# End of the first feed-forward: operand parts ahead of the squares, and the next stage's first unit copied unscaled

## Chip, cores and metric

The kernel runs on one core of one Trainium2 chip. The metric is the device time of one execution in microseconds (us), as the median of several runs. The engines are called PE (matmul; PEld is its weight load), DVE (VectorE), ACT (ScalarE), POOL (GpSimd) and SP (which here only issues DMAs).

## What is computed

Two transformer blocks follow each other on one sequence of 1024 tokens with 1024 features, all in fp32. The change touches the seam between them, where the first block's feed-forward ends, its last norm is taken, and the second block's input projection begins:

```python
        h2 = rmsnorm(x, norm_ffn[l])
        gate, up = jnp.split(h2 @ w_ffn_in[l], 2, axis=-1)
        x = x + (jax.nn.silu(gate) * up) @ w_ffn_out[l]
    return rmsnorm(x, norm_final)
...
    for l in range(DEPTH):
        a = rmsnorm_2(x, norm_pre_mix[l])
        mix = token_mixer(a, cos, sin, w_in[l], b_gates[l], conv_w[l], conv_b[l], ml_head_norm[l],
                          q_norm[l], w_uq[l], kv_norm[l], w_ukv[l], w_out[l])
...
def token_mixer(a, cos, sin, w_in, b_gates, conv_w, conv_b, ml_head_norm,
                q_norm, w_uq, kv_norm, w_ukv, w_out):
    proj = a @ w_in
```

## The kernel before

Activations lie transposed: `acc` holds x as eight tiles of 128 features by 1024 tokens. Every fp32 product is made of three matmuls on split operands: high weight part by high operand part, high by low, low by high. The high part of an operand is a rounded copy, the low part is the value less the high part.

**The feed-forward's output.** It is done in "pairs" of output tiles by a Strassen-like scheme of seven products (`r` = 0 to 6). The last pair is `P1_LAST`. `output_dve` adds the products into `acc`; `f1_act` makes high weight parts and, between them, squares.

**The seam.** `FIN = (5, 6, 7, 0, 1, 2, 4, 3)` is the order in which the tiles of `acc` are finished; number n of it is called "tile n" here (0 to 7). Each tile needs four things:

- `fin_squares` (ACT): two squares, one plain into `sq_a`, one with the last norm's gain into `sq_b`. Each buffer exists once, so a square waits until DVE has added the one before it.
- `fin_add` (DVE): the "A add" of `sq_a` into `sq_sum_a`, and the "B add" of `sq_b` into `sq_sum_b`.
- `fin_hi` (ACT): the high operand part `g1hi`.
- `fin_lo` (DVE): the low operand part `g1lo`.

`fin_pe` sums the squares over the features by matmuls with ones (`ones,sq_sum_a`, then `ones,sq_sum_b`). `fin_means` (DVE) turns the sums into means and reciprocals, and writes them on diagonals. `fin_spread` (PE) spreads these over the partitions, and `fin_act` takes the roots `r1` (tile name `lat_r`) and `rstd`. The two norms follow each other, so one pair of sums serves both.

**The next stage.** `in2` projects in 17 "units" of one output tile each, 48 matmuls of 128x512, in the order of `IN2_ORDER`. Unit 0 has buffers of its own for its weights; the others alternate between two. `split_unit` makes a unit's high and low weight parts on POOL and waits until the unit two before it is done on PE. `store_dve` multiplies a unit's result in PSUM by `rstd` into `stage`, which frees the PSUM banks; `store_act` stores it. `fin_dve` then scales the eight tiles of `acc` (L2310), `spill2_act` writes all of `acc` to HBM as one DMA (`x_block<-acc`), and SP waits for that DMA in `gates_sp` before it issues six small loads and then the weights of unit 5:

```python
                if j == 4:
                    gates_sp(sp)
...
        def gates_sp(sp):
            sp.wait_ge(S["x_spilled"], 32)
            sp.wait_ge(S["stored"][U_IN2 % 2], stored2(0))
```

The order on each engine is the order of the code; engines meet at semaphores only.

Of the kernel before, what the change touches and what calls it, by code (L numbers as in the profile page):

```python
# [18 lines left out]
ALU = mybir.AluOpType  # L19
# [178 lines left out]
def parted(m):  # L198

    return PARTED_TO[m]  # L200
# [99 lines left out]
def two_block_kernel(nc, A, out):  # L300
# [34 lines left out]
    with ctx:  # L335
# [1702 lines left out]
        def f1_act(act):  # L2038
# [32 lines left out]
            for p in range(2, P2):  # L2071
                first_act(act, p)
                for i in range(7):
                    pair_act(act, p, i)
                    change_act(act, p, i)
                    if p < P1O and p % 2 == 0 and i in (3, 4, 5):
                        silu_act(act, p // 2, i - 3)
                    if P1_LAST - 3 < p and i in (1, 4):
                        fin_squares(act, 2 * (p - P1_LAST + 2) + i // 4)
                if p < P1O and p % 2 == 0:  # L2080
                    silu_act(act, p // 2, 3)
            for n in range(KT):
                fin_hi(act, n)
# [51 lines left out]
        def f1_dve(dve):  # L2135
# [35 lines left out]
            for n in range(4, KT):  # L2171
                fin_lo(dve, n)
            for n in (KT - 2, KT - 1):
                fin_add(dve, n)
# [76 lines left out]
        def fin_act(act):  # L2251
            for n in (KT - 2, KT - 1):
                fin_squares(act, n)
            f = 2 * NORM_AT["final"]
            act.wait_ge(S["norm_sum"], f + 3)
            act.activation(r1, PS[2][:, :], ACT.Sqrt).then_inc(S["rstd_ready"], 1)
            act.wait_ge(S["norm_sum"], f + 4)
            act.activation(rstd[:, :], PS[3][:, :], ACT.Sqrt).then_inc(S["rstd_ready"], 1)

        def in2_weights_pool(pool, i):  # L2260
# [9 lines left out]
            else:  # L2270
                pool.wait_ge(*count("sw_lo", parted(AT[P1_LAST, 6])))
                pool.wait_ge(*count("s_product", done(P1_LAST, 3)))
                split_unit(pool, u)

# [28 lines left out]

        FIN0 = KT + 3

# [66 lines left out]
        def in2_pe(pe):  # L2372
            pe.wait_ge(*count("s_post", posted(P1_LAST - 1, "12")))
            for j in range(N_IN2):
                if j == 0:
                    mm_unit(pe, Step(U_IN2), g1hi, g1lo, ks=FIN, w=(whi_in2, wlo_in2), wait_k=lambda k:
                            pe.wait_ge(S["lo_ready"], OPERAND["mix2"] + FIN.index(k) + 1))
                else:
                    mm_unit(pe, Step(U_IN2 + j), g1hi, g1lo,
                            wait_k=(lambda k: fin_spread(pe) if k == 3 else None) if j == 1 else None)  # L2380
                if j == 0:
                    fin_pe(pe)
                if j == 8:
# [16 lines left out]
        def in2_act(act):  # L2400
            for j in range(N_IN2):
                t = IN2_ORDER[j]
                store_act(act, Step(U_IN2 + j), proj2[t * P:(t + 1) * P, :])
                if j == 0:
                    spill2_act(act)
                if j == 2:
                    gates_act(act)
# [27 lines left out]
        def in2_dve(dve):  # L2435
            dve.wait_ge(S["rstd_ready"], NORM_AT["mix2"] + 1)
            for j in range(N_IN2):
                store_dve(dve, Step(U_IN2 + j), U_IN2, B2)
                if j == 0:
                    fin_dve(dve)  # L2440
# [1578 lines left out]
        def output_dve(dve, p):  # L4019
# [52 lines left out]
            next_lo(dve, p, 3)  # L4072
            if P1_LAST - 3 < p < P2:
                fin_add(dve, 2 * (p - P1_LAST + 2))
            if N_PAIR - 4 < p:
                end_adds(dve, p - 1)
# [17 lines left out]
            next_lo(dve, p, 5)  # L4094
            if p == P1_LAST:
                for n in range(3):
                    fin_lo(dve, n)
            change_dve(dve, p, 6)
# [5 lines left out]
            change_dve(dve, p, 7)  # L4104
            if P1_LAST - 3 < p < P2:
                fin_add(dve, 2 * (p - P1_LAST + 2) + 1)
# [303 lines left out]
```

## Time and profile before

| what | value |
|---|---|
| median of 3 runs | 2695.09 us (2694.74 to 2695.11) |
| profiled execution, own time | 2693.12 us |
| span of the profile | 2691.4 us |
| mean granted PE clock, share of full | 0.994 |
| busy: PE, DVE, POOL, ACT | 2595.1, 1857.9, 1224.1, 1042.9 us |

The span runs from the first to the last instruction. Times in the rows are from the span's start. A row's brackets give the idle time of that engine just before, and what ended it.

### The profile page before, as it was taken

The numbers are of one execution on the slowest core, as the hardware profiler recorded it, in microseconds if no ns is written. First come the engines' busy times: TensorE is split into PE (matmuls) and PEld (weight loads), VectorE is DVE, ScalarE is ACT, GpSimd is POOL, SyncE is SP. The second block draws the span as 40 slices with busy tenths as digits, with TensorE's granted clock in tenths as the row PEclk, the third lists the DMA queues.
The fourth block names the chain that finished last, engine by engine and source line by source line (L and its number), as shares of the span: only waits on it lengthen the run. The fifth ranks groups of instructions, "written<-read, shape, count | busy, mean of one in ns | idle before, by whom it ended". The sixth has DMA issues, their size and how long they took to land.

```text
span 2691.4 us, 32407 instructions
## 1 busy us (share of the span) xinstructions
PE 2595.1 (96%) x12366; PEld 2089.7 (78%) x12366; DVE 1857.9 (69%) x2108; ACT 1042.9 (39%) x1447; POOL 1224.1 (45%) x763
## 2 busy tenths in 40 slices
PE   7999999999999999999998999989998999999998
PEld 5888787887777888887886788656885888877777
DVE  7565665457658666668879647766558666778887
ACT  5223343323124333234435111756555433434444
POOL 2222222233447888884333433241135888723331
PEclk9999999999999999999999999999999999999999
DMA  5333333244332433245641343401323554754543
GB/s 192 118 102 114 121 94 126 83 152 155 130 130 63 118 102 111 81 133 199 215 137 55 132 152 101 126 1 46 131 83 84 172 155 147 220 156 160 164 141 141
DMA packets 335840, 339.49 MB, mean 126 GB/s; under 512 B 19723, under 2 KB 254838, under 8 KB 335686
## 3 DMA queue, kind: packets, MB, share of 16 engines
q1 hardware_dynamic: 329446, 313.81, 37.3%
q10 hardware_dynamic: 6240, 23.59, 2.3%
q8 instruction: 100, 1.64, 0.2%
q14 instruction: 54, 0.44, 0.1%
HBM read 228.55 MB, written 107.77 MB: 125 GB/s over the span
## 4 chain that ended last, share of the span: by engine, by line
PE 52%; DVE 10%; issue 2%; ACT 1%; DMA 1%; POOL 1%; SPq 0%; DVEq 0%; ACTq 0%; POOLq 0%
PE ps L3712 36%; PE ps L566 9%; DVE op_lo L3789 2%; PE ps L2784 2%; PE ps L2807 1%; DVE sw_lo L3622 1%; PE ps L2794 1%; DVE acc L4033 1%; DVE acc L4040 1%; PE ps L3288 1%; DVE acc L2310 0%; DVE x L2731 0%; DMA x_block<-acc 0%; DVE op_lo L3692 0%; PE ps L3673 0%
## 5 line engine op out<-in xcount | busy, mean ns | idle before, releaser
L3712 PE MATMUL ps<-op_hi,sw_hi 128*128 128x512 f32 x1769 | 693.2, 392 | 15.8 <-DVE op_lo L3789 8.4
L3712 PE MATMUL ps<-op_hi,sw_lo 128*128 128x512 f32 x1769 | 689.7, 390 | 0.0
L3712 PE MATMUL ps<-op_lo,sw_hi 128*128 128x512 f32 x1769 | 689.5, 390 | 0.0
L3712 PEld LDWEIGHTS ps<-op_hi,sw_hi 128*128 128x128 f32 x1769 | 332.8, 188 | 96.6 <-issue 16.7
L3712 PEld LDWEIGHTS ps<-op_hi,sw_lo 128*128 128x128 f32 x1769 | 332.8, 188 | 69.7
L3712 PEld LDWEIGHTS ps<-op_lo,sw_hi 128*128 128x128 f32 x1769 | 333.0, 188 | 68.9 <-issue 0.5
L532 POOL TENSOR_TENSOR w_hi_t<-w_raw,ones 128x1024 fp32r<-128x1024 f32 (+1 forms) x60 | 118.5, 1978 | 531.1 <-DMA w_raw<-in_w_in 238.0
L3612 ACT ACTIVATE sw_hi<-sw_sumNone 128x512 fp32r<-128x512 f32 (+1 forms) x252 | 157.1, 624 | 332.2 <-PE ps L3712 250.0
L3622 POOL TENSOR_TENSOR sw_lo<-sw_sumNone,sw_hi 128x512 fp32r<-128x512 f32 x138 | 213.8, 1559 | 34.2 <-ACT sw_hi L3612 34.1
L3573 POOL TENSOR_TENSOR sw_sumNone<-sw_raw 128x512 f32<-128x512 f32 (+1 forms) x63 | 113.8, 1806 | 232.1 <-DVE sw_lo L3622 209.3
L3612 ACT ACTIVATE sw_hi<-sw_raw 128x512 fp32r<-128x512 f32 (+1 forms) x189 | 117.5, 622 | 198.1 <-PE ps L3712 196.4
L3622 POOL TENSOR_TENSOR sw_lo<-sw_raw,sw_hi 128x512 fp32r<-128x512 f32 x109 | 159.2, 1462 | 54.7 <-ACT sw_hi L3612 54.7
L536 POOL TENSOR_TENSOR w_lo_t<-w_raw,w_hi_t 128x1024 fp32r<-128x1024 f32 (+1 forms) x60 | 156.3, 2609 | 4.2
L674 DVE TENSOR_TENSOR stage<-ps,rstd 128x1024 f32<-128x1024 f32 x37 | 45.1, 1219 | 125.3 <-PE ps L566 110.1
L3588 POOL TENSOR_TENSOR sw_sumNone<-sw_raw,sw_sumNone 128x512 f32<-128x512 f32 (+1 forms) x63 | 91.7, 1456 | 87.5 <-DVE sw_lo L3622 84.8
L3744 DVE TENSOR_TENSOR hidden_blocks<-ps,s_u 128x512 f32<-128x512 f32 x111 | 76.1, 686 | 77.4 <-PE ps L3712 76.9
L3580 POOL TENSOR_TENSOR sw_sumNone<-sw_sumNone,sw_raw 128x512 f32<-128x512 f32 (+1 forms) x63 | 98.7, 1566 | 61.8 <-DVE sw_lo L3622 59.0
L3728 DVE TENSOR_TENSOR s_u<-ps,s_p 128x512 f32<-128x512 f32 x65 | 44.8, 689 | 116.3 <-PE ps L3712 111.1
L3789 DVE TENSOR_TENSOR op_lo<-op_raw,op_hi 128x2048 fp32r<-128x2048 f32 (+1 forms) x49 | 119.1, 2433 | 7.2 <-ACT op_hi L3782 7.2
L566 PE MATMUL ps<-m2hi,w_hi_t 128*128 128x512 f32 x304 | 106.1, 405 | 3.7 <-DVE m2lo L1450 2.1
L566 PE MATMUL ps<-h1hi,w_hi_t 128*128 128x512 f32 x320 | 103.7, 405 | 4.0 <-DVE stage L674 4.0
L566 PE MATMUL ps<-m2lo,w_hi_t 128*128 128x512 f32 x304 | 101.7, 390 | 0.0
(500 smaller groups left out, 5423.5 us busy)
## 6 DMA issues: line engine op xcount, KB each, us to landing
op_raw<-hidden SPq DMA_DIRECT2D x42, 1024.0 KB, 8.7
w_raw<-in_w_in SPq DMA_DIRECT2D x47, 512.0 KB, 4.6
sw_raw<-in_w_ffn_in SPq DMA_DIRECT2D x44, 512.0 KB, 5.2
hidden<-hidden_blocks SPq DMA_DIRECT2D x13, 1536.0 KB, 6.1
hidden<-hidden_blocks SPq DMA_DIRECT2D x14, 1280.0 KB, 5.0
sw_raw<-in_w_up SPq DMA_DIRECT2D x32, 512.0 KB, 8.6
sw_raw<-in_w_down SPq DMA_DIRECT2D x32, 512.0 KB, 5.5
acc<-proj SPq DMA_DIRECT2D x30, 512.0 KB, 4.5
```

The lines of the kernel that those rows point to most:

```text
L532: ins = pool.tensor_tensor(whi[:, u.par, s], raw[:, u.par, s], ones[:, 0:1].to_broadcast([P, n]), ALU.mult)
L536: ins = pool.tensor_tensor(wlo[:, u.par, s], raw[:, u.par, s], whi[:, u.par, s].bitcast(F32), ALU.subtract)
L566: mm = pe.matmul(out[:, b * HALF:(b + 1) * HALF], w, x[:, k, b * HALF:(b + 1) * HALF], start=(begin and k == ks[0] and n == 0), stop=(end ...
L2784: mm = pe.matmul(PS[n % 2][:, b:b + w], qT[0:96, h, i * P:(i + 1) * P], kT[0:96, h, b:b + w], start=True, stop=True)
L3573: pool.tensor_tensor(s1, a21, a22, ALU.add).then_inc(S["sw_sum"], 1)
L3580: pool.tensor_tensor(s2, s1, a11, ALU.subtract).then_inc(S["sw_sum"], 1)
L3588: pool.tensor_tensor(s2, a12, s2, ALU.subtract).then_inc(S["sw_sum"], 1)
L3612: act.activation(wshi[ring(m)][:, 0:n], weight_block(p, r), ACT.Copy).then_inc(S["sw_hi"], 1)
L3622: eng.tensor_tensor(wslo[ring(m)][:, 0:n], weight_block(p, r), wshi[ring(m)][:, 0:n].bitcast(F32), ALU.subtract).then_inc(S["sw_lo"], 1)
L3712: mm = pe.matmul(out, w, x[:, k, :], start=(k == 0 and i == 0 and r < 4), stop=(k == n - 1 and i == 2), skip_group_check=r >= 4)
L3744: dve.tensor_tensor(out, bank(p, r), u[:, :], ALU.add).then_inc(S["s_post"], 1)
L3789: dve.tensor_tensor(lo_of(first, r)[:, :, :], fresh_of(first, r)[:, :, :], hi_of(first, r)[:, :, :].bitcast(F32), ALU.subtract).then_inc(S ...
```

## The change

On ACT, the high parts of the first three tiles are made inside the last pair, where tile 4's squares stood. After the pair come tile 4's squares, the high weight part of unit 1 (which POOL made before; POOL now only makes its low part), the other five high parts, and then the squares of tiles 5 to 7. On DVE, the first three low parts follow the third addition of the last pair, where tile 4's adds stood; the other five follow the pair's end, and all adds of tiles 4 to 7 come behind them. On PE, the sums stand no longer between units 0 and 1 but ahead of the sixth of unit 1's eight contraction steps, and the spreads ahead of the second step of unit 2 instead of the fourth of unit 1. Unit 0 is copied unscaled from PSUM by ACT (`in2_copy`); DVE scales it in `stage` later (`in2_scaled`), after it has stored unit 1 and before `fin_dve`.

```diff
-                    if P1_LAST - 3 < p and i in (1, 4):
+                    if P1_LAST - 3 < p < P1_LAST and i in (1, 4):
                         fin_squares(act, 2 * (p - P1_LAST + 2) + i // 4)
+                    if (p, i) == (P1_LAST, 1):
+                        for n in range(3):
+                            fin_hi(act, n)
                 if p < P1O and p % 2 == 0:
                     silu_act(act, p // 2, 3)
-            for n in range(KT):
+            fin_squares(act, 4)
+            in2_weights_act(act)
+            for n in range(3, KT):
                 fin_hi(act, n)
...
             for n in range(4, KT):
                 fin_lo(dve, n)
-            for n in (KT - 2, KT - 1):
+            for n in range(4, KT):
                 fin_add(dve, n)
...
         def fin_act(act):
-            for n in (KT - 2, KT - 1):
+            for n in range(5, KT):
                 fin_squares(act, n)
+            in2_copy(act)
...
-                pool.wait_ge(*count("sw_lo", parted(AT[P1_LAST, 6])))
-                pool.wait_ge(*count("s_product", done(P1_LAST, 3)))
-                split_unit(pool, u)
+                split_lo(pool, u)
+
+        def in2_weights_act(act):
+            act.wait_ge(S["w_split"], U_IN2 + 1)
+            act.wait_ge(*count("sw_lo", parted(AT[P1_LAST, 6])))
+            act.wait_ge(*count("s_product", done(P1_LAST, 3)))
+            split_hi(act, Step(U_IN2 + 1))
+
+        def in2_copy(act):
+
+            u = Step(U_IN2)
+            act.wait_ge(S["unit_done"], U_IN2 + 1)
+            act.wait_ge(S["stored"][u.par], stores_before(u, U_IN2, B2) * 16)
+            act.activation(stage[:, u.par, :], PS[u.par][:, :], ACT.Copy).then_inc(S["unit_out"][u.par], 1)
+
+        def in2_scaled(dve):
+
+            u = Step(U_IN2)
+            dve.wait_ge(S["unit_out"][u.par], u.nth())
+            dve.tensor_tensor(stage[:, u.par, :], stage[:, u.par, :], rstd[:, :], ALU.mult).then_inc(S["fin_done"], 1)
...
                     mm_unit(pe, Step(U_IN2 + j), g1hi, g1lo,
-                            wait_k=(lambda k: fin_spread(pe) if k == 3 else None) if j == 1 else None)
-                if j == 0:
-                    fin_pe(pe)
+                            wait_k={1: lambda k: fin_pe(pe) if k == 5 else None,
+                                    2: lambda k: fin_spread(pe) if k == 1 else None}.get(j))
...
-                store_act(act, Step(U_IN2 + j), proj2[t * P:(t + 1) * P, :])
                 if j == 0:
+                    u = Step(U_IN2)
+                    act.wait_ge(S["fin_done"], FIN0)
+                    act.dma_start(proj2[t * P:(t + 1) * P, :], stage[:, u.par, :]).then_inc(S["stored"][u.par], 16)
                     spill2_act(act)
+                else:
+                    store_act(act, Step(U_IN2 + j), proj2[t * P:(t + 1) * P, :])
...
-            for j in range(N_IN2):
+            for j in range(1, N_IN2):
                 store_dve(dve, Step(U_IN2 + j), U_IN2, B2)
-                if j == 0:
+                if j == 1:
+                    in2_scaled(dve)
                     fin_dve(dve)
...
-            if P1_LAST - 3 < p < P2:
+            if P1_LAST - 3 < p < P1_LAST:
                 fin_add(dve, 2 * (p - P1_LAST + 2))
+            if p == P1_LAST:
+                for n in range(3):
+                    fin_lo(dve, n)
...
-            if p == P1_LAST:
-                for n in range(3):
-                    fin_lo(dve, n)
...
-            if P1_LAST - 3 < p < P2:
+            if P1_LAST - 3 < p < P1_LAST:
                 fin_add(dve, 2 * (p - P1_LAST + 2) + 1)
```

`split_hi` and `split_lo` are there before; `split_hi` is one ACT copy of 128x1024, `split_lo` one subtraction of that size on POOL. `FIN0` grows by one for the new step.

Three places of the order on the engines follow. The first is DVE at the end of the last pair, from tile 4's adds to the last adds; `acc<-ps,acc` are the pair's additions, `g1lo` the low parts, `sq_sum_a` and `sq_sum_b` the adds. Before:

```order
L2243 TENSOR_TENSOR sq_sum_a<-sq_sum_a,sq_a 128x1024
L2249 TENSOR_TENSOR sq_sum_b<-sq_sum_b,sq_b 128x1024
L4040 TENSOR_TENSOR acc<-ps,acc 128x512 x2
L2232 SCALAR_TENSOR_TENSOR g1lo<-acc,gg,g1hi 128x1024 x3
L4040 TENSOR_TENSOR acc<-ps,acc 128x512
L2243 TENSOR_TENSOR sq_sum_a<-sq_sum_a,sq_a 128x1024
L2249 TENSOR_TENSOR sq_sum_b<-sq_sum_b,sq_b 128x1024
L2232 SCALAR_TENSOR_TENSOR g1lo<-acc,gg,g1hi 128x1024 x5
L2243 TENSOR_TENSOR sq_sum_a<-sq_sum_a,sq_a 128x1024
L2249 TENSOR_TENSOR sq_sum_b<-sq_sum_b,sq_b 128x1024
L2243 TENSOR_TENSOR sq_sum_a<-sq_sum_a,sq_a 128x1024
L2249 TENSOR_TENSOR sq_sum_b<-sq_sum_b,sq_b 128x1024
```

The same place after the change, from the third addition of the last pair on:

```order
L4067 TENSOR_TENSOR acc<-ps,acc 128x512
L2237 SCALAR_TENSOR_TENSOR g1lo<-acc,gg,g1hi 128x1024 x3
L4067 TENSOR_TENSOR acc<-ps,acc 128x512 x3
L2237 SCALAR_TENSOR_TENSOR g1lo<-acc,gg,g1hi 128x1024 x5
L2248 TENSOR_TENSOR sq_sum_a<-sq_sum_a,sq_a 128x1024
L2254 TENSOR_TENSOR sq_sum_b<-sq_sum_b,sq_b 128x1024
L2248 TENSOR_TENSOR sq_sum_a<-sq_sum_a,sq_a 128x1024
L2254 TENSOR_TENSOR sq_sum_b<-sq_sum_b,sq_b 128x1024
L2248 TENSOR_TENSOR sq_sum_a<-sq_sum_a,sq_a 128x1024
L2254 TENSOR_TENSOR sq_sum_b<-sq_sum_b,sq_b 128x1024
L2248 TENSOR_TENSOR sq_sum_a<-sq_sum_a,sq_a 128x1024
L2254 TENSOR_TENSOR sq_sum_b<-sq_sum_b,sq_b 128x1024
```

The low parts moved to the front and all eight adds to the back; how many of each there are is unchanged.

The second place is DVE at the first stores of `in2`, from the second diagonal on; `stage<-ps,rstd` is `store_dve`, `acc<-acc,cols,lat_r` is `fin_dve`. Before:

```order
L614 TENSOR_TENSOR lat_r<-ident,bytok 128x1024
L674 TENSOR_TENSOR stage<-ps,rstd 128x1024
L2310 SCALAR_TENSOR_TENSOR acc<-acc,cols,lat_r 128x1024 x8
L674 TENSOR_TENSOR stage<-ps,rstd 128x1024 x3
L2562 MEMSET ssq 4x1024
```

After the change:

```order
L614 TENSOR_TENSOR lat_r<-ident,bytok 128x1024
L674 TENSOR_TENSOR stage<-ps,rstd 128x1024
L2296 TENSOR_TENSOR stage<-stage,rstd 128x1024
L2333 SCALAR_TENSOR_TENSOR acc<-acc,cols,lat_r 128x1024 x8
L674 TENSOR_TENSOR stage<-ps,rstd 128x1024 x2
L2589 MEMSET ssq 4x1024
```

One row is new, L2296, ahead of the eight; the store ahead of it is now unit 1's.

The third place is ACT from the last pair's middle on; `sw_hi_106` is the last high weight part of the feed-forward, `w_hi_t` unit 1's. After the change:

```order
L2231 ACTIVATE g1hi<-acc,gg 128x1024 x3
L3639 ACTIVATE sw_hi_106<-sw_sumNone_122 128x384
L2222 ACTIVATE sq_a<-acc 128x1024
L2224 ACTIVATE sq_b<-acc,cols 128x1024
L542 ACTIVATE w_hi_t<-w_raw 128x1024
L2231 ACTIVATE g1hi<-acc,gg 128x1024 x5
L2222 ACTIVATE sq_a<-acc 128x1024
L2224 ACTIVATE sq_b<-acc,cols 128x1024
L2222 ACTIVATE sq_a<-acc 128x1024
L2224 ACTIVATE sq_b<-acc,cols 128x1024
L2222 ACTIVATE sq_a<-acc 128x1024
L2224 ACTIVATE sq_b<-acc,cols 128x1024
```

Before, all eight high parts stood together behind the squares of tiles 4 and 5, and there was no row for `w_hi_t`.

## Rows read from the trace of the kernel before

**Rows 1.** Page of the profile: busy time, share, instructions of the matmul engine

```profile
PE 2595.1 (96%) x12366; PEld 2089.7 (78%) x12366; DVE 1857.9 (69%) x2108; ACT 1042.9 (39%) x1447; POOL 1224.1 (45%) x763
```

**Rows 2.** Timeline of PE, 1455 to 1520: start, duration (us), what, [idle before, releaser]

```profile
1466.61 0.39 PE L3712 MATMUL ps<-op_hi,sw_lo 128*128 128x512 f32 x1
...
1473.50 1.19 PE L566 MATMUL ps<-g1hi,w_hi_in 128*128 128x512 f32 x2 [6.50 <-DVE g1lo L2232]
...
1479.86 0.73 PE L566 MATMUL ps<-g1hi,w_hi_in 128*128 128x512 f32 x2 [0.59 <-DVE g1lo L2232]
...
1488.19 2.05 PE L602 MATMUL ps<-ones,sq_sum_a 128*128 128x128 f32 x16 [1.24 <-DVE sq_sum_a L2243]
...
1491.02 2.05 PE L602 MATMUL ps<-ones,sq_sum_b 128*128 128x128 f32 x16 [0.78 <-DVE sq_sum_b L2249]
...
1492.83 0.71 PE L566 MATMUL ps<-g1hi,w_hi_t 128*128 128x512 f32 x2
...
1497.01 1.88 PE L608 MATMUL ps<-ssq,ones 128*128 128x512 f32 x4
```

**Rows 3.** Timeline of DVE, 1455 to 1520

```profile
1464.32 2.12 DVE L2243 TENSOR_TENSOR sq_sum_a<-sq_sum_a,sq_a 128x1024 f32<-128x1024 f32 x1
...
1466.37 3.38 DVE L2249 TENSOR_TENSOR sq_sum_b<-sq_sum_b,sq_b 128x1024 f32<-128x1024 f32 x1
...
1472.07 3.67 DVE L2232 SCALAR_TENSOR_TENSOR g1lo<-acc,gg,g1hi 128x1024 fp32r<-128x1024 f32 x3 [1.13 <-ACT g1hi L2226]
...
1478.53 6.06 DVE L2232 SCALAR_TENSOR_TENSOR g1lo<-acc,gg,g1hi 128x1024 fp32r<-128x1024 f32 x5
...
1486.91 1.22 DVE L2243 TENSOR_TENSOR sq_sum_a<-sq_sum_a,sq_a 128x1024 f32<-128x1024 f32 x1
...
1501.70 1.23 DVE L674 TENSOR_TENSOR stage<-ps,rstd 128x1024 f32<-128x1024 f32 x1 [5.39 <-ACT rstd L2258]
...
1502.84 13.46 DVE L2310 SCALAR_TENSOR_TENSOR acc<-acc,cols,lat_r 128x1024 f32<-128x1024 f32 x8
```

**Rows 4.** Timeline of POOL, 1430 to 1600

```profile
1463.09 2.28 POOL L532 TENSOR_TENSOR w_hi_t<-w_raw,ones 128x1024 fp32r<-128x1024 f32 x1 [6.10 <-DVE sw_lo L3622]
...
1465.45 3.21 POOL L536 TENSOR_TENSOR w_lo_t<-w_raw,w_hi_t 128x1024 fp32r<-128x1024 f32 x1
...
1487.10 2.78 POOL L532 TENSOR_TENSOR w_hi_t<-w_raw,ones 128x1024 fp32r<-128x1024 f32 x1 [18.44 <-PE ps L566]
...
1509.03 2.86 POOL L532 TENSOR_TENSOR w_hi_t<-w_raw,ones 128x1024 fp32r<-128x1024 f32 x1
...
1518.44 1.89 POOL L532 TENSOR_TENSOR w_hi_t<-w_raw,ones 128x1024 fp32r<-128x1024 f32 x1 [3.23 <-PE ps L566]
...
1520.42 2.39 POOL L536 TENSOR_TENSOR w_lo_t<-w_raw,w_hi_t 128x1024 fp32r<-128x1024 f32 x1
```

**Rows 5.** Timeline of ACT, 1455 to 1520

```profile
1470.84 8.41 ACT L2226 ACTIVATE g1hi<-acc,gg 128x1024 fp32r<-128x1024 f32 x8
```

**Rows 6.** Chain that ended last, 1500 to 1760: start, us, what

```profile
1516.33 11.73 DMA x_block<-acc
...
1531.30 4.10 DMA w_raw<-in_w_in
...
1535.47 2.38 POOL w_hi_t L532
...
1540.36 43.81 PE ps L566 x192
```

**Rows 7.** Timeline of PE: two other waits of over 2 us

```profile
750.97 0.72 PE L566 MATMUL ps<-m1hi,w_hi_t 128*128 128x512 f32 x2 [2.59 <-POOL w_lo_t L536]
...
1267.86 0.47 PE L3712 MATMUL ps<-op_hi,sw_hi 128*128 128x512 f32 x1 [2.54 <-DVE op_lo L3789]
```

**Rows 8.** Stretches: PEclk is the granted clock, 1.00 is full

```profile
1268.50:1271.90 3.40, 3.40 (x10) 2.62 (x9) 2.32 (x3) 0.00 (x0) 1.28 (x1) 0.51 1.11 344
...
1470.00:1476.50 6.50, 3.00 (x7) 2.48 (x8) 5.37 (x7) 6.50 (x7) 0.00 (x0) 0.50 0.27 76
```

More of the change, by code:

```diff
@@ L2302, in fin_means @@
             diagonal(dve, ssq2, 1).then_inc(S["norm_mean"], 2)
-        FIN0 = KT + 3
+        FIN0 = KT + 4
         def fin_dve(dve):
```

## Prediction

> **What bounds the kernel now.** The page comes first: PE is busy 2595.1 of 2691.4 us [rows 1], so a time saved elsewhere counts only where PE waits. The timeline of PE shows where it does at the seam. The feed-forward ends at 1466.61 + 0.39 = 1467.0, and PE then stands idle for 6.50 us, until DVE has the first low part. There follow 0.59 us before tile 3, 1.24 us before the A sums and 0.78 us before the B sums [rows 2], 9.1 us in all. After the wait the granted clock is at 0.50, which is 1.2 GHz, from 1470 to 1476.5 [rows 8]; some 3 us of work at half clock cost another 1.6.
>
> The timeline of DVE says why the low parts are late: tile 4's adds start at 1464.32 and 1466.37 and take 2.12 and 3.38 us [rows 3] where such an add takes 1.22 (1486.91). POOL is splitting unit 1's weights from 1463.09 to 1465.37 and from 1465.45 to 1468.66 [rows 4]; each add ends 1.1 us after POOL's instruction, so it had stood still until POOL was through. The eight scalings of `fin_dve` show the same: 13.46 us [rows 3], where eight at the 1.2 us of a low part (6.06 for five) make 9.6; POOL's 1509.03 and the one behind it fall into them [rows 4]. A split that waits for nobody holds DVE for 1.89 + 2.39 = 4.28 us (1518.44 and 1520.42) [rows 4].
>
> The chain of waits gives the last thing to read, and it decides. `fin_dve` ends at 1516.3, the write of `acc` starts at 1516.33 and lands 11.7 us later, SP issues its small loads, unit 5's weights land from 1531.30 on, POOL splits them at 1535.47, and PE starts unit 5 at 1540.36 [rows 6]. So unit 5 starts 24.03 us after `fin_dve` is done, however early PE gets there. PE came only 0.3 us too early: units 3 and 4 are 48 matmuls each, 10.9 us a unit (1540.36 + 43.81 for 192, which are four), and unit 2 was done when POOL started at 1518.44 [rows 4, 6], so unit 4 was done at about 1540.1.
>
> **Part by part.** First, PE's stall. With the first high parts made inside the last pair, the first low part needs only DVE, free at 1464.32. ACT makes unit 1's high weights when DVE has parted the last feed-forward weights, which released POOL at 1463.09 [rows 4]; at 8.41/8 = 1.05 us a copy [rows 5] POOL can take the low part at 1464.25. It may hold DVE for 2.39 us; if DVE gets in first, the second low part is held instead. In the first case low parts 0 to 2 end at 1467.9, 1469.1 and 1470.2; three additions of 0.6 us (my reading of the 0.6 between such rows) bring 1472.0, and low part 3 ends at 1473.3. PE starts at 1467.95, waits 1.3 us before tile 3, and from there needs what it needed before, 1479.86 to 1487.0 [rows 2]: unit 0 is done at 1480.4, 6.6 us earlier. Both waits are short; I take no fall of the clock there.
>
> Second, the sums. PE reaches the sixth step of unit 1 at 1480.4 + 5 x 1.36 = 1487.2 (6 matmuls of 0.227 us a step, from 43.81/192). When is the last A add done? Between 1464.32 and that add DVE does the same work before and after: eight low parts, three additions, seven adds. Before it ended at 1486.91 + 1.22 = 1488.13, and the stretch held three waits: 0.9 and 2.2 us for POOL, 1.13 idle [rows 3], 4.2 in all. Now it holds unit 1's low part, 2.39, and, because unit 0 is done at 1480.4, unit 2's whole split, 4.28, which before started at 1487.10 [rows 4], behind all but one add: 6.67, less nothing idle, since ACT's squares for tiles 5 to 7 take turns with the adds and hide beside them (0.1 us at most). The last A add ends 6.67 - 4.2 = **2.5 us later**, at 1490.6, and PE stands idle for 3.4 us before the sums.
>
> Third, the spreads. Sums cost 1.81 us each (1491.02 to 1492.83) [rows 2]. Before, from the last A add to the spreads: 1497.01 - 1488.13 = 8.9. Now: two sums 3.6, then four steps 5.45, and a start of 0.1: 9.1. The B adds and the diagonals fit beside the four steps. **+0.2**.
>
> Fourth, roots to the write. The spreads to `rstd` stay 1497.01 to 1501.70 [rows 2, 3]. DVE then stores unit 1 (1.14, as unit 0 before), scales unit 0, which is new: **+1.14**, and runs the eight scalings. Unit 3's split is over by then, but unit 4's starts when unit 2 is done, about 6 us into the eight, just where unit 3's fell before, so they keep 13.46. `in2_copy` (1 us on ACT) hides beside the sums on PE. The Trainium skill bears on this edit ("SBUF — State Buffer", "SBUF: two separate sides"): a DVE instruction with two SBUF inputs and a POOL instruction exclude each other for the whole instruction. By that rule the scaling in `stage`, unlike the one from PSUM, could be held by a split, up to 4.28 us more if it met one; I count no hold, as POOL is free then by the rows.
>
> So `fin_dve` ends 2.5 + 0.2 + 1.14 = **3.84 us later**, and with it unit 5's start. What PE gained is spent in front of unit 5, where it now stands idle for some 9 us.
>
> Fifth, the clock. Of two waits of like length, 2.54 us was followed by 3.4 us at 0.51 and 2.59 us by none [rows 7, 8]. For the 3.4 us before the sums the price is 0 or 3.4/2 = 1.7; I take **+1.7**, the longer wait being nearer to the fall. For the 9 us before unit 5 a fall is as good as certain; what it costs lies between 0 (the clock is back as the work starts) and 3.4 (the whole 6.5 us at 0.50 on work); I take what the 6.50 us wait cost, **+1.6**.
>
> Sum: 3.84 + 1.7 + 1.6 = +7.1 us on the profiled execution's own 2693.12 (its span is 2691.4), 2700.2. The median of the runs lies 1.97 above it, 2695.09, so **2702.2**, 0.26% slower. Behind unit 5 everything hangs on PE and moves with it.
>
> **The rivals.** What a measurement of this kernel can tell from no change is about 0.2%, 5.4 us: 2689.7 to 2700.5.
>
> *Late write, cheap clock.* The same chain, but the clock holds at the sums, or is back when unit 5 starts: +3.8 to +5.5, 2698.9 to 2700.6. For it stands the 2.59 us wait without a fall. Chance 0.28.
>
> *POOL's split does not meet the adds.* If the adds slip through between POOL's instructions, the last A add ends at 1486.1 and PE is not held: the spreads come at 1487.2 + 9.1 = 1496.3, 0.7 earlier, the scaling takes its 1.14, and the write starts 0.5 later; with the clock's 1.6, +2.1, 2697.2. Against it stand all four held DVE rows. Chance 0.1.
>
> *The write is not what unit 5 waits for* (the other side). If the 24.03 us from write to unit 5 shrank by 9 us or more, PE's own progress would count: after the sums PE has done 6.8 us more work than at 1492.83, and it is there at 1490.6 + 3.6 = 1494.2: 5.4 us gained, less 0 to 1.7 for the clock, so 2689.7 to 2691.4. The 0.3 us with which unit 5 waited before speaks for a balance of the two; but nothing in the change touches the DMA, the small loads or POOL's split. Below 9 us of shrinking the gain is less, and over 0.2% it is only if the A adds come earlier too. Chance 0.07.
>
> **How the numbers follow.** The forecast, late write with both falls of the clock, has 0.52 and its own range 2700.6 to 2704.6 (1.8 us more than forecast if the second fall costs 3.4, and 0.6 for the terms before it). 0.03 is left for a worse meeting of splits with the scalings (+4.3 more). The range reaches down to the third case: 2697.0 to 2704.6. Slower by over 0.2%: 0.52 + 0.03 = 0.55. Within: 0.28 + 0.1 and 0.02 of the last rival = 0.4. Faster: the other 0.05 of it.
>
> **What the changed profile would show.** Right: PE's wait before unit 0 falls from 6.50 us to about 1; unit 2's split on POOL starts near 1480.5, and an A and a B add beside it are held for about 2 us each; the A sums start near 1490.6 after an idle time of about 3 us; the write of `acc` starts at 1520 to 1522; PE idles 9 to 10 us before unit 5, released by POOL's low part, at 1544 to 1546, with a clock of 0.50 around it. Wrong: a write before 1516.3, or a unit 5 that waits for nothing. The step that I trust least is the meeting of POOL's and DVE's instructions, since an order that differs by 0.1 us moves 2 us.

## The result, and the profile after

The changed kernel takes 2701.07 us, the median of 17 runs (2697.52 to 2703.15), against 2694.74 us for 17 runs of the kernel before on the same chip: ratio 1.0024, 95% interval 1.0017 to 1.0031, so 6.3 us slower. 2702.2 was predicted. A profile is of one execution and need not be the median's: this one is of the fastest of the 17.

The timeline of PE in the profile after (own time 2697.52 us) answers to [rows 2]:

```profile
1461.57 0.50 PE L3739 MATMUL ps<-op_hi,sw_hi 128*128 128x512 f32 x1 [0.53 <-DVE s_u L3762]
...
1466.84 0.70 PE L566 MATMUL ps<-g1hi,w_hi_in 128*128 128x512 f32 x2 [0.89 <-DVE g1lo L2237]
...
1472.13 0.73 PE L566 MATMUL ps<-g1hi,w_hi_in 128*128 128x512 f32 x2 [0.93 <-DVE g1lo L2237]
...
1489.05 2.05 PE L602 MATMUL ps<-ones,sq_sum_a 128*128 128x128 f32 x16 [3.02 <-DVE sq_sum_a L2248]
1490.94 1.95 PE L602 MATMUL ps<-ones,sq_sum_b 128*128 128x128 f32 x16
...
1498.19 1.88 PE L608 MATMUL ps<-ssq,ones 128*128 128x512 f32 x4
...
1542.24 1.22 PE L566 MATMUL ps<-g1hi,w_hi_t 128*128 128x512 f32 x2 [9.16 <-POOL w_lo_t L536]
```

The stall before unit 0 has shrunk from 6.50 to 0.89 us, and two others have grown: 3.02 us before the A sums and 9.16 us before unit 5, which was 0.30 us before. To compare executions I count from the first row here, the last pair's matmul that waits for `s_u`. Call it R. It comes between 1459.9 and 1464.3 in the profiles of this document, whatever the kernel, so times from the span's start can't be laid beside each other. It and the end of the stretch read so in the kernel before (the timelines of PE and of POOL):

```profile
1462.60 0.50 PE L3712 MATMUL ps<-op_hi,sw_hi 128*128 128x512 f32 x1 [0.54 <-DVE s_u L3735]
```

```profile
1551.68 2.08 POOL L532 TENSOR_TENSOR w_hi_t<-w_raw,ones 128x1024 fp32r<-128x1024 f32 x1 [4.21 <-PE ps L566]
```

The second row is POOL's start on unit 7, which PE releases by finishing unit 5: 89.08 us after R. DVE after, which answers to [rows 3]:

```profile
1463.30 5.79 DVE L2237 SCALAR_TENSOR_TENSOR g1lo<-acc,gg,g1hi 128x1024 fp32r<-128x1024 f32 x3
...
1480.35 2.89 DVE L2254 TENSOR_TENSOR sq_sum_b<-sq_sum_b,sq_b 128x1024 f32<-128x1024 f32 x1
1483.17 3.42 DVE L2248 TENSOR_TENSOR sq_sum_a<-sq_sum_a,sq_a 128x1024 f32<-128x1024 f32 x1
...
1487.77 1.23 DVE L2248 TENSOR_TENSOR sq_sum_a<-sq_sum_a,sq_a 128x1024 f32<-128x1024 f32 x1
...
1502.88 1.23 DVE L674 TENSOR_TENSOR stage<-ps,rstd 128x1024 f32<-128x1024 f32 x1 [7.82 <-ACT rstd L2264]
1504.03 1.22 DVE L2296 TENSOR_TENSOR stage<-stage,rstd 128x1024 f32<-128x1024 f32 x1
1505.16 13.43 DVE L2333 SCALAR_TENSOR_TENSOR acc<-acc,cols,lat_r 128x1024 f32<-128x1024 f32 x8
```

And POOL after, which answers to [rows 4]:

```profile
1463.20 2.40 POOL L546 TENSOR_TENSOR w_lo_t<-w_raw,w_hi_t 128x1024 fp32r<-128x1024 f32 x1 [7.24 <-ACT w_hi_t L542]
1479.38 2.79 POOL L532 TENSOR_TENSOR w_hi_t<-w_raw,ones 128x1024 fp32r<-128x1024 f32 x1 [13.77 <-PE ps L566]
1482.24 3.26 POOL L536 TENSOR_TENSOR w_lo_t<-w_raw,w_hi_t 128x1024 fp32r<-128x1024 f32 x1
...
1511.47 2.70 POOL L532 TENSOR_TENSOR w_hi_t<-w_raw,ones 128x1024 fp32r<-128x1024 f32 x1 [8.66 <-PE ps L566]
1514.25 3.25 POOL L536 TENSOR_TENSOR w_lo_t<-w_raw,w_hi_t 128x1024 fp32r<-128x1024 f32 x1
1537.54 1.89 POOL L532 TENSOR_TENSOR w_hi_t<-w_raw,ones 128x1024 fp32r<-128x1024 f32 x1 [20.03 <-DMA w_raw<-in_w_in]
...
1555.30 1.89 POOL L532 TENSOR_TENSOR w_hi_t<-w_raw,ones 128x1024 fp32r<-128x1024 f32 x1 [5.93 <-PE ps L566]
```

Laid over each other, these two show the mechanism. POOL's split of unit 2 starts at 1479.38 because unit 0 is done then, and beside it a B add takes 2.89 us and an A add 3.42 us where the undisturbed one takes 1.23. POOL's own two take 2.79 and 3.26 us there. The chain that ended last, after, goes where that of before went [rows 6]:

```profile
1518.62 11.75 DMA x_block<-acc
...
1533.61 3.87 DMA w_raw<-in_w_in
...
1537.54 1.89 POOL w_hi_t L532
...
1539.51 2.68 POOL w_lo_t L536
...
1542.24 45.55 PE ps L566 x192
```

The stretch from R to the end of unit 5 now takes 1555.30 - 1461.57 = 93.73 us, 4.65 more than before; this profiled execution has no fall of the clock at the sums. Where those 4.65 us come from is plain in PE's waits and its clock: before 6.50 + 0.59 + 1.24 + 0.78 + 0.30 and 1.6 for half clock, 11.0 us; after 0.89 + 0.93 + 3.02 + 9.16 and 1.74, 15.7 us. The rest, PE's work, is the same 78 us in both.

### The profile page after: what moved, and what is told of

Read it like the earlier page. It is cut to its first block, busy times and chain, and to the rows that moved or that the text cites. A ratio compares the mean times of both kernels' runs of the same rounds, so it can differ in the third digit from the quotient of the medians.

```text
span 2695.8 us, 32408 instructions
## 1 busy us (share of the span) xinstructions
PE 2595.4 (96%) x12366; PEld 2090.2 (78%) x12366; DVE 1854.4 (69%) x2108; ACT 1045.7 (39%) x1449; POOL 1219.1 (45%) x762
## 4 chain that ended last, share of the span: by engine, by line
PE 53%; DVE 9%; issue 2%; DMA 2%; ACT 1%; POOL 1%; SPq 0%; DVEq 0%; ACTq 0%; POOLq 0%
PE ps L3739 36%; PE ps L566 9%; DVE op_lo L3816 2%; PE ps L2811 2%; PE ps L2834 1%; PE ps L2821 1%; DVE sw_lo L3649 1%; DMA op_raw<-hidden 1%; PE ps L3315 1%; DVE acc L4060 1%; DVE acc L4067 0%; DVE x L2758 0%; DVE acc L2333 0%; DMA x_block<-acc 0%; DVE sq_sum_a L2248 0%
```

## The experiments

Two theories stood against each other. **W**: unit 5's start hangs on the write of `acc`, so only what moves the write counts. **S**: the loss is the new wait at the sums with its half clock, and the write is a bystander. The table gives what the profiles show, all from R: when the write of `acc` is issued, when unit 5 starts and how long PE had waited for it, when unit 5 is done; the last column is the median less that of before in the same batch.

| kernel | wait at A sums | write | unit 5 (wait) | unit 5 done | median, us |
|---|---|---|---|---|---|
| before | 1.24 | 53.73 | 77.76 (0.30) | 89.08 | |
| changed | 3.02 | 57.05 | 80.67 (9.16) | 93.73 | +6.33 |
| e10, changed again | 3.01, clock falls | 58.49 | 82.17 (9.22) | 94.84 | +6.85 |
| e3, unit 2's split held | 0 | 53.78 | 77.73 (9.49) | 91.55 | +1.91 |
| e1, unit 4's split held | 2.98, clock falls | 54.91 | 78.52 (5.37) | 91.52 | +3.31 |
| e12, both held | 0 | 49.97 | 73.64 (5.44) | 87.58 | -1.56 |
| e8, first half alone | 9.77, clock falls | 55.96 | no wait | 90.99 | +1.88 |
| e9, before, write held | 1.23 | 56.75 | 80.42 (2.93) | 94.51 | +3.49 |
| e11, first half, waits moved | 6.05, clock falls | 48.91 | no wait | 87.44 | -0.63 |
| e5, all waits moved | 0 | 49.96 | no wait | 79.22 | -10.94 |

**e1: unit 4's split held until the eight scalings are done.** In `in2_pool`:

```diff
+                if j == 4:
+                    pool.wait_ge(S["fin_done"], FIN0 + KT)
                 if j >= 2:
                     split_unit(pool, Step(U_IN2 + j))
```

> The changed kernel, with POOL's split of unit 4's weights held back until the eight scalings of fin_dve are done. Nothing ahead of the scalings moves, PE's 3.0 us wait before the sums included. Theory W (unit 5 starts a fixed 23.6 us after the write of acc is issued, and the cost is that the write comes later): the scalings take 9.4 us instead of 13.4, the write is issued at about 1514.6 instead of 1518.6, PE's wait before unit 5 shrinks from 9.2 to about 5.2 us, and the time falls by 4.0 us against the changed kernel, to 2.3 us above before (ratio 1.0008). Theory S (the cost is PE's own wait and low clock at the sums, and the wait before unit 5 only shows time already lost): no change, 6.3 us above before (1.0024).

2697.84 us, ratio 1.0011 (1.0003 to 1.0020): 3.0 us less than the changed kernel lost, where W had said 4.0. DVE's timeline:

```profile
1507.53 9.65 DVE L2333 SCALAR_TENSOR_TENSOR acc<-acc,cols,lat_r 128x1024 f32<-128x1024 f32 x8
```

The scalings fall from 13.43 to 9.65 us, the wait before unit 5 from 9.16 to 5.37, by the same 3.8. The wait at the sums is the same 2.98 us, and here the clock did fall, seen in the length of the A sums' row on PE:

```profile
1489.78 3.68 PE L602 MATMUL ps<-ones,sq_sum_a 128*128 128x128 f32 x16 [2.98 <-DVE sq_sum_a L2248]
```

Half the loss goes though nothing at the sums became better: for W, against S.

**e3: unit 2's split held until the adds are done**, `if j == 2: pool.wait_ge(S["fin_done"], KT)` at the same place.

> The changed kernel, with POOL's split of unit 2's weights held back until the last B add. Theory W: the adds are no longer held, the last A add ends at about 1485.1 instead of 1489.0, PE goes from unit 1's fifth step into the sums without its 3.0 us wait, the spreads and the write come 3.0 us earlier (write at 1515.6), and the time falls by 3.0 us, and by up to 1.7 more where the clock fell at the sums: 1.6 to 3.3 us above before (1.0006 to 1.0012), with some 6 us of wait left before unit 5 and more of PE's gain unused. Theory S: the wait at the sums was the cost, so with it gone the kernel is as fast as before or faster (1.0000 or less).

2696.44 us, ratio 1.0005 (0.9997 to 1.0014). PE's timeline (A sums, unit 5):

```profile
1488.67 1.95 PE L602 MATMUL ps<-ones,sq_sum_a 128*128 128x128 f32 x16
...
1542.07 1.22 PE L566 MATMUL ps<-g1hi,w_hi_t 128*128 128x512 f32 x2 [9.49 <-POOL w_lo_t L536]
```

No wait at the sums at all, so POOL's split was the whole of it, and yet PE waits 9.49 us before unit 5. Counted from R the write (53.78) and unit 5 (77.73) are where they were in the kernel before (53.73, 77.76): what PE gained earlier is handed back to within 0.1 us. W had said some 6 us of wait; it stays at 9, since PE reaches unit 5 earlier by as much as the write comes earlier. The 2.47 us that are left until unit 5 is done are the half clock after that wait. S asked for a ratio of 1.0000 or less here, and the time doesn't exclude it: of the eleven executions five took 2693.1 to 2694.0 us and six 2696.4 to 2698.8. The profile, of the slowest, speaks against S; what the five faster ones lacked no profile shows.

**e8: the first half of the change alone.** Operand parts ahead of the squares as in the change, but the sums between units 0 and 1, the spreads in unit 1, and unit 0 stored from PSUM, as before.

```diff
-            in2_copy(act)
...
-                            wait_k={1: lambda k: fin_pe(pe) if k == 5 else None,
-                                    2: lambda k: fin_spread(pe) if k == 1 else None}.get(j))
+                            wait_k=(lambda k: fin_spread(pe) if k == 3 else None) if j == 1 else None)
+                if j == 0:
+                    fin_pe(pe)
```

> The first half of the change alone: operand parts ahead of the squares, unit 1's high weights on ACT; but the sums stay between units 0 and 1, the spreads ahead of unit 1's fourth step, and DVE scales and stores unit 0 from PSUM as before. Theory W: the last A add comes as late as in the changed kernel, so PE waits about 10 us before the sums; from there two sums and three steps to the spreads, and no scaling in stage: the write comes 1.2 us later than before, 2.9 with a fall of the clock at the sums, and so does the end: 1.0004 to 1.0011. What the changed kernel loses beyond this is the price of the second half. If earlier operand parts help by themselves, it is faster than before.

2696.76 us, ratio 1.0008 (0.9999 to 1.0017). PE's timeline:

```profile
1488.19 3.48 PE L602 MATMUL ps<-ones,sq_sum_a 128*128 128x128 f32 x16 [9.77 <-DVE sq_sum_a L2248]
```

The last A add is as late as in the whole change (27.4 us after R in both), so the first half already spends PE's gain: it waits the 9 us at the sums instead of at unit 5. The second half moves that wait behind the write and makes the write later by 2.5 us (58.49 in e10 against 55.96): 1.1 for the scaling in `stage`, 1.4 for one contraction step more between the sums and the spreads, four instead of three. It costs 4.4 us by the medians (of two batches). By the stretch to unit 5's end it costs 3.9 (94.84, e10, which like e8 has the clock's fall at the sums); 93.73, without the fall, would give 2.7.

**e2: the kernel before with unit 3's split held** until the scalings are done (`j == 3`, the split that meets them there).

> The kernel before, with POOL's split of unit 3's weights held back until the eight scalings are done. The write of acc is issued about 4 us earlier, at 1512.3 instead of 1516.3. Theory W with PE only 0.3 us early at unit 5: at most 0.3 us is gained (ratio 0.9999), since PE's own progress takes over; the 0.3 us wait before unit 5 is gone. If the write's time counted alone in the kernel before too: 4 us gained (0.9985).

2692.74 us, ratio 0.9995 (0.9986 to 1.0004). The scalings take 9.68 us, the write comes 49.99 us after R instead of 53.73, and unit 5 waits for nothing. It is done 88.51 us after R instead of 89.08, 0.6 us earlier, where the wait that it had to gain was 0.3, and the ratio's interval holds 1. In the kernel before, write and PE were in balance, which is why a write 3.3 us later shows and one 3.7 us earlier doesn't.

**e4: unit 5's weights ahead of the small loads.** In `in2_sp` of the changed kernel:

```diff
-                if j == 4:
+                if j == 5:
                     gates_sp(sp)
```

> The changed kernel, with SP loading unit 5's weights ahead of its wait for the write of acc and the six small loads, which now stand ahead of unit 6's weights. The write itself stays where it is. Theory W: unit 5 starts at about 1533 without a wait. DVE's chain on the small loads (the gates, then the store of unit 4, which ended at 1548.3) is the next thing that hangs on the write: unit 6 waits for it until about 1548.4, instead of starting near 1554.6; with a clock fall after that shorter wait 5 to 6 us are gained on the changed kernel, which puts it 0.3 to 1.5 us above before (1.0001 to 1.0006). Theory S: nothing is gained, 1.0024.

2698.04 us, ratio 1.0013 (1.0004 to 1.0022): direction right, size above what W said. The wait before unit 5 is gone, but the gate work on DVE, which waits for the small loads and so now stands later, is still ahead of unit 4's store, and unit 6 writes into the buffer which that store empties:

```profile
1552.21 0.71 PE L566 MATMUL ps<-g1hi,w_hi_t 128*128 128x512 f32 x2 [3.65 <-DVE stage L674]
```

In its profile unit 5's 9.2 us have become 3.65 here, and the stretch is 0.9 us longer than before (1599.13 less R at 1464.28, against 1596.51 less 1462.60, the same start of POOL four units on); the median says 3.5, where W had said 0.3 to 1.5. The profile is of this kernel's slowest execution, which lost another 4.9 us behind the seam, with more falls of the clock there: the mean granted clock is 0.90 in the 50 us from 250 us after R and 0.97 in those from 900 us on, where it was 0.97 and 1.00 before. Why, I did not find out.

**e6: the gate work of the kernel before one unit later**, on all three engines:

```diff
-                if j == 4:
+                if j == 5:
                     gates_sp(sp)
...
-                if j == 2:
+                if j == 3:
                     gates_act(act)
...
-                if j == 3:
+                if j == 4:
                     gates_dve(dve)
-                if j == 4:
+                if j == 5:
                     rows_dve(dve)
```

> The kernel before with only the moves of the small loads and of the work on them (unit 5's weights first, the work one unit later on ACT and DVE), and nothing of the change. Theory W: PE's own progress bounds it, so only the 0.3 us wait before unit 5 goes: 0.9999, within 0.03% of before. If these moves alone made the gain of a kernel that has them all, it shows here: 0.997.

2693.88 us, ratio 0.9995 (0.9986 to 1.0004). The interval holds W's 0.9999 and not the 0.997 of the other case. In the profile the last 0.3 us of waiting goes, and unit 5 is done 88.51 us after R as in e2. The hold of e2 and these moves were not run together on the kernel before; each alone leaves PE nothing to wait for up to unit 5's end.

**e5: the changed kernel with everything that W names removed**: both holds (e1, e3) and the three moves of e6.

> The changed kernel with both splits held back (unit 2's until the last B add, unit 4's until the eight scalings are done), unit 5's weights loaded ahead of the small loads, and the work on the small loads one unit later on ACT and DVE (behind the stores of units 3 and 4, its second part behind unit 5's), so that no store of a unit stands behind it. Theory W: the waits before the sums, before unit 5 and before unit 6 are all gone, the write is issued at about 1511.5, and PE runs without a wait of over 0.5 us from unit 0's fourth step to the end of the 17 units; unit 6 starts some 9 us earlier than in the kernel before. 7 to 10 us faster than before (ratio 0.9963 to 0.9974). If something else than the write and its chain holds the units (DMA bandwidth, POOL's splits), less than 4 us are gained.

2683.94 us, the median of five executions, ratio 0.9963 (0.9950 to 0.9975): 10.9 us less than before, slightly more than W gave, where the changed kernel took 6.3 more: 17.2 us (0.6%) between the two. PE's timeline of the whole stretch holds these waits and no other:

```profile
1466.04 0.70 PE L566 MATMUL ps<-g1hi,w_hi_in 128*128 128x512 f32 x2 [0.88 <-DVE g1lo L2237]
...
1471.33 0.73 PE L566 MATMUL ps<-g1hi,w_hi_in 128*128 128x512 f32 x2 [0.95 <-DVE g1lo L2237]
...
1485.07 1.95 PE L602 MATMUL ps<-ones,sq_sum_a 128*128 128x128 f32 x16
```

and its table by stretches says the same of the clock (PEclk, third column from the end):

```profile
1460.00:1545.00 85.00, 82.65 (x372) 66.87 (x371) 60.73 (x54) 23.24 (x21) 31.19 (x16) 1.00 0.47 155
```

So the change could save 9.9 us in this stretch (89.08 - 79.22), and what held it back were POOL's two splits and the place of the gate work with its small loads. From R to the end of the span this execution is 7.4 us shorter than the one before: 2.5 us are lost again behind the stretch, where the granted clock is 0.90 against 0.97 in the 50 us from 250 us after R.

**e7: the kernel before with a later write, first try.** Three more copies on ACT ahead of the write in `spill2_act`:

```diff
             act.wait_ge(S["fin_done"], FIN0 + KT)
+            for i in range(3):
+                act.activation(lat_s[:, i, :], rstd[:, :], ACT.Copy)
             act.dma_start(tile_of(x2_d, 0, KT), acc[:, :, :]).then_inc(S["x_spilled"], 16)
```

> The kernel before with three more ACT copies of 128x1024 between the end of the scalings and the write of acc: the write is issued 3.1 us later, at about 1519.5, and nothing on DVE, PE or POOL is touched. Theory W: unit 5 starts 2.9 us later than before, at about 1543.2, after a wait of 3.1 us; with a fall of the clock or without one 2.9 to 4.5 us slower (1.0011 to 1.0017). Theory S (the write's time does not set the end): within 0.5 us of before (1.0000 to 1.0002).

2694.64 us, ratio 0.9998 (0.9989 to 1.0007). This is no verdict on W, since the write did not move. ACT's timeline, with its queue:

```profile
1515.10 1.06 ACT L2316 ACTIVATE lat_s<-rstd 128x1024 f32<-128x1024 f32 x1 [14.66 <-DVE acc L2310]
1515.11 0.38 ACTq L2317 DMA_DIRECT2D x_block<-acc  x1
1516.07 1.04 ACT L2316 ACTIVATE lat_s<-rstd 128x1024 f32<-128x1024 f32 x1
```

The DMA was issued 0.01 us after the first copy started, although three copies stand ahead of it in the code.

**e9: the same, with the write waiting for the copies.**

```diff
             act.wait_ge(S["fin_done"], FIN0 + KT)
+            for i in range(3):
+                act.activation(lat_s[:, i, :], rstd[:, :], ACT.Copy).then_inc(S["fin_done"], 1)
+            act.wait_ge(S["fin_done"], FIN0 + KT + 3)
             act.dma_start(tile_of(x2_d, 0, KT), acc[:, :, :]).then_inc(S["x_spilled"], 16)
```

> The kernel before, with the write of acc held back: three more copies of 128x1024 on ACT stand ahead of it, each raises the semaphore, and the write waits for the third, so it is issued about 3.1 us later (three times 1.03 us). Nothing else moves, the sums least of all. W (the write's time fixes unit 5): unit 5 starts about 2.8 us later behind a wait of about 3.1 us on POOL's low part; with 0 to 1.7 us for a fall of the clock after it +2.8 to +4.5 us, ratio 1.0010 to 1.0017. S (what is lost is lost at the sums): no change, 1.0000.

2698.37 us, ratio 1.0015 (1.0006 to 1.0024), inside what W gave. The chain that ended last shows it whole:

```profile
1521.09 11.74 DMA x_block<-acc
...
1536.08 3.87 DMA w_raw<-in_w_in
...
1540.02 1.94 POOL w_hi_t L532
...
1542.04 2.68 POOL w_lo_t L536
```

A write 3.0 us later makes unit 5 start 2.7 us later, behind a wait of 2.93 us, and nothing at the sums differs (1.23 against 1.24 us). This speaks for W against S: the write alone, moved by about as much as the change moves it in the first profile, costs over half of what the change costs. The other part this run doesn't show. (The profile is of this kernel's slowest execution, 2702.47 us, so its 94.51 lies above what the median says.)

**e10: the changed kernel again**, with e9, e11 and e12 on one chip.

> The changed kernel itself once more, beside e9, e11 and e12 on one chip. Both theories: 1.0017 to 1.0031 as the first time; write near 56 to 57 us after PE's first matmul that waits for DVE's operand sum in the last pair, and 9 us of waiting before unit 5. Whether the clock falls at the sums is open.

2701.73 us, ratio 1.0025 (1.0015 to 1.0034). This profile does have the fall at the sums:

```profile
1490.82 3.49 PE L602 MATMUL ps<-ones,sq_sum_a 128*128 128x128 f32 x16 [3.01 <-DVE sq_sum_a L2248]
```

```profile
1490.80:1494.00 3.20, 3.18 (x15) 3.18 (x16) 1.14 (x1) 2.07 (x2) 0.00 (x0) 0.52 0.10 11
```

The second fence is its table by stretches: a granted clock of 0.52 in the sums. The write then comes 1.44 us later than in the first profile, 58.49 us after R where 56 to 57 was said, and unit 5 is done 5.76 us later than before instead of 4.65.

**e12: the changed kernel with both splits held**, gate work where it was.

> The changed kernel with both of POOL's splits held (unit 2's until the adds are done, unit 4's until the eight scalings are done) and nothing else moved; e5 without the gate work moved. W: the two holds add up, 4.3 + 3.8 = 8.1 us off the write's time, so the write comes some 4.5 us before that of before, and unit 5 still waits for it, 24 us behind; the falls of the clock at the sums (1.7) goes. Against before: -4.5 + 0 to 1.7: ratio 0.9983 to 0.9990, with 4 to 6 us of waiting left before unit 5, which only e5's moved gate work removes. If the waits were not in this chain: 0.9963 as e5.

2693.32 us, ratio 0.9996 (0.9987 to 1.0004), above the 0.9983 to 0.9990 that W gave. The write comes 3.8 us before that of before, where W said 4.5, and unit 5 4.1 us earlier; but only 1.5 us arrive at unit 5's end. The wait of 5.44 us has put the clock down, and unit 5 takes 13.94 us from its start to its end, where before it took 11.32. Half clock cost 2.6 us here, and I had allowed 0 to 1.7.

**e11: e5 without the second half of the change** (e8's sums and stores, with unit 2's and unit 3's splits held and the gate work moved).

> The first half of the change alone (operand parts ahead of the adds, sums between units 0 and 1 as before, unit 0 stored from PSUM), with unit 2's split held until the adds are done, unit 3's split held until the eight scalings are done, and the gate work one unit later as in e5. It is e5 without the unscaled copy and without sums inside unit 2. W: the write is no longer what unit 5 waits for, so PE's waits count: PE waits about 5.5 us before the A sums (9.8 less the 4.3 of the split), where e5 waits for nothing, and a fall of the clock there costs another 1.7; so e5's 0.9963 plus 5.5 to 7.2 us: 0.9983 to 0.9990. If the second half of the change were worth nothing once the write comes early: 0.9963.

2694.25 us, ratio 0.9996 (0.9987 to 1.0005), 10.3 us above e5 (of another batch), and above the 0.9983 to 0.9990 that W gave. PE's timeline:

```profile
1487.58 3.78 PE L602 MATMUL ps<-ones,sq_sum_a 128*128 128x128 f32 x16 [6.05 <-DVE sq_sum_a L2248]
```

Unit 5 is done 8.2 us later than in e5: 6.05 of waiting at the sums, the rest, 2.2, half clock. I had said 5.5 to 7.2. The second half of the change, which costs about 4 us as it was made, is worth these 8.2 us once the write comes early.

## Why the prediction was right

The time, 2701.07 against 2702.2, came by the steps that were named. From R, so that the executions can be compared:

- **PE's stall, right.** 0.89 us before unit 0 (about 1 was said), 0.93 before tile 3 (1.3). Unit 0 is done 17.8 us after R, where 17.9 was said (1480.5 less 1462.60).
- **The sums, right in kind, 0.6 us too much.** The last A add ends 27.43 us after R instead of 25.53: +1.9, where 2.5 was said. I had charged DVE with POOL's full 2.39 and 4.28 us. The rows give 5.79 for three low parts that take 3.67 alone, 2.1 us, and 2.89 + 3.42 - 2 x 1.22 = 3.9 us for the two adds: each held instruction lost 0.2 to 0.3 us less than POOL's own time. Why, no run shows. e3, where the meeting is taken away, has no wait at all.
- **The spreads, +0.31** (9.19 us from the last A add to the spreads, 8.88 before) where 0.2 was said.
- **The scaling in `stage`, right.** From the spreads to the write 20.43 us instead of 19.32, +1.11 (1.14 was said): L2296 starts at 1504.03 and the eight 1.13 us behind it, and they keep their 13.43. The Trainium skill ("SBUF — State Buffer", "SBUF: two separate sides") has DVE instructions with two SBUF inputs and POOL's that read SBUF exclude each other for the whole instruction; this case's held adds agree (2.89 and 3.42 us against 1.23), and so does e1, where the scalings fall to 9.65 us as POOL's split leaves them. Whether the scaling in `stage` can be held no run shows: it took 1.22 us in every kernel that has it, and no split fell on it.
- **The write, +3.32 from R** (3.84 was said), and from there to unit 5 23.62 us instead of 24.03, because POOL's first part took 1.89 us and not 2.37 and the load 3.87 instead of 4.10, while POOL's second part took 2.67 instead of 2.39. So unit 5 came 2.9 us later, not 3.84. The wait before it is 9.16 us (about 9 was said). That the write fixes it, e9, e1 and e3 show, each from another side.
- **The clock, the term that varies.** At the sums I took 1.7 us of 0 to 1.7. After a wait of 3.02 us there was none; of 3.01, 2.98 and 3.04 us (e10, e1, e4) there was one, the A sums taking 3.49 to 3.68 us instead of 2.05. At unit 5, 1.6 was said. From unit 5's start to its end it is 11.32 us before and 13.06 after, +1.74; in e10 1.35, and over the other kernels with that wait 1.7 (e1), 2.5 (e3), 2.6 (e12) and 2.8 (e9). The changed kernel's table by stretches shows why the number is not fixed:

```profile
1536.00:1542.20 6.20, 0.00 (x0) 0.00 (x0) 4.46 (x5) 5.57 (x5) 4.58 (x3) 0.50 0.67 209
1542.20:1543.00 0.80, 0.76 (x2) 0.67 (x3) 0.80 (x1) 0.00 (x0) 0.80 (x1) 0.50 0.00 0
...
1545.00:1546.00 1.00, 1.00 (x4) 0.81 (x3) 1.00 (x1) 0.00 (x0) 0.92 (x2) 0.55 0.28 78
1546.00:1547.00 1.00, 1.00 (x6) 0.80 (x5) 1.00 (x1) 0.00 (x0) 1.00 (x1) 1.00 0.00 0
```

PE stopped at 1533.1; the clock fell to 0.50, 1.2 GHz, at 1535.7 and stayed there through the rest of the idle time and for another 3.7 us of work, half of which is lost. In all six profiles it was low before the work began, and it stayed low for 3.0 (e10), 3.7 (changed, e1), 5.4 (e3), 5.6 (e12) and 5.9 us (e9) of work; half of that is the price above to within 0.2 us. So the price is what is left of the low stretch when PE starts, and not a matter of the wait's length alone: 2.93 us of waiting (e9) cost more than 9.16.

The sum by measured terms is 1.90 + 0.31 + 1.11 - 0.41 + 1.74 = 4.65 without a fall at the sums, and 5.76 were measured in the profile that has one. The medians say 6.3 and 6.9. From R to the end of the span the two profiles are 5.4 and 6.5 us longer than the one before, so 0.7 to 0.8 us are lost behind the stretch, where the forecast had everything move with unit 5. The granted clock is 0.93 there in both, against 0.97 before, in the 50 us from 250 us after R; what of this belongs to the change I can't assign. The forecast's 7.1 us by terms stands against 5.8 in e10's stretch: 0.9 too much on the start of unit 5, 0.3 on the clock at the sums and 0.3 on the clock at unit 5, while the 0.7 us behind the stretch were not forecast. That the median came within 1.2 us of 2702.2 is in part luck, since these misses offset each other.

Two numbers of the forecast were worked out wrongly, and neither changes it: a whole 6.5 us of work at half clock cost 3.25 us and not 3.4, and in the rival where the split does not meet the adds the last A add ends at 1486.3 (1488.13 - 4.2 + 2.39) and not 1486.1.

Of the rivals, the late write with a cheap clock is what the first profile shows (+3.8 to +5.5 was its range), so forecast and rival were one mechanism, and executions lie on both sides. POOL's split did meet the adds. The other side needed the way from write to unit 5 to shrink by 9 us, and it shrank by 0.4; e5 shows what that side is worth when it is made to.

## What to carry to other kernels

Before an idle time is closed, follow the next stage's start back along the chain of waits: if it hangs on a write, a load and a split that the edit doesn't move, the idle time goes there, and it may cost a second fall of the clock. A matmul engine that is early also releases its helpers early, and a split that starts earlier can hold the vector work on which the chain depends; here two waits on a semaphore, and one group of loads and the work on them placed a unit later, turned 6.3 us lost into 10.9 us won. Where an edit has two halves, time them apart, and again after the chain is loosened: the second half cost about 4 us as it was made and was worth 8 in the loosened chain.

## What I had not expected of the hardware

- A DMA on ACT's queue does not wait for the ACT instructions ahead of it unless a semaphore says so: issued 0.01 us after the first of three copies had started, and 0.96 and 1.91 us before the other two did (e7), and 3.0 us later once it waited for them (e9).
- Waits of almost one length are followed by a fall of the clock or not: 3.02 us without, 2.98, 3.01 and 3.04 us with.
- Where POOL and DVE meet, both are stretched: POOL's 1.89 us part takes 2.79, and 2.39 takes 3.26, while DVE's 1.22 take 2.89 and 3.42. It looks as if the two engines took turns, one instruction each: the B add ends 1.07 us after POOL's first part, and POOL's second part 2.26 us after the B add.
